# Splitting the log decays of a gated linear attention into three bf16 parts before their products with 0/1 matrices

## The reference, cut to what matters

```
z = einsum('bnsr,srk->bnsk', lr, w_gk) + b_gk
log_a = log_sigmoid(z) / GLA_GATE_NORM            # two directions, 4 heads x 64 channels
...
bc = cumsum(log_a within a chunk)
diff = bc[..., :, None, :] - bc[..., None, :, :]
decay = exp(where(causal, diff, -inf))
attn = sum(q[..., :, None, :] * k[..., None, :, :] * decay, axis=-1)
```

## Time and profile before

| | us |
|---|---|
| median of 3 runs (1561.78, 1561.84, 1566.01) | 1561.84 |
| the profiled execution | 1566.27 |
| its span, first to last instruction | 1564.6 |
| PE busy | 1421.5 (91%) |
| DVE busy | 425.7 (27%) |
| ACT busy | 261.4 (17%) |
| POOL busy | 133.6 (9%) |

### The profile page before, as it was taken

The page is one execution under the profiler, slowest core; times in us unless marked ns, Lnnn a source line. Parts: engine busy times, 40 slices in busy tenths (PEclk is TensorE's granted clock), DMA queues, the critical chain, the costliest instruction groups (busy, mean ns, idle before and its releaser), DMA issues. The chain is left out here.

```text
span 1564.6 us, 28137 instructions
## 1 busy us (share of the span) xinstructions
PE 1421.5 (91%) x11994; PEld 742.3 (47%) x11995; DVE 425.7 (27%) x1058; ACT 261.4 (17%) x489; POOL 133.6 (9%) x357
## 2 busy tenths in 40 slices
PE   3899988899999999999959998979998999999996
PEld 2675656434434434444446666554443444344442
DVE  2291774311111111111125538460111111111112
ACT  1313204211101111101113231141111111111110
POOL 2600631000000000000000026020000000000000
PEclk8899999899999999999979999979999999999998
DMA  6854950599999999999745679009999999999994
GB/s 248 276 186 173 362 185 1 234 420 420 420 420 409 416 420 420 421 415 421 325 161 177 239 267 318 29 7 421 421 421 420 421 418 413 414 400 421 420 416 177
DMA packets 114116, 507.48 MB, mean 324 GB/s; under 512 B 14880, under 2 KB 20796, under 8 KB 64572
## 3 DMA queue, kind: packets, MB, share of 16 engines
q1 hardware_dynamic: 113372, 504.43, 80.5%
q0 software_dynamic: 384, 1.05, 0.2%
q10 hardware_dynamic: 224, 0.06, 0.0%
HBM read 503.41 MB, written 2.10 MB: 323 GB/s over the span
## 5 line engine op out<-in xcount | busy, mean ns | idle before, releaser
L971 PE MATMUL ps<-ring,h 128*32 128x512 f32 x2720 | 374.8, 599 | 24.1 <-DMA ring<-in_exp_w_up 14.8
L971 PEld LDWEIGHTS ps<-ring,h 128*32 128x32 f32 x2720 | 109.3, 111 | 248.5 <-issue 248.5
L990 PE MATMUL ps<-ring,work 128*32 128x512 f32 x1360 | 199.6, 598 | 3.1 <-DVE store L1627 1.6
L971 PE MATMUL ps<-store,h 128*32 128x512 f32 x608 | 191.1, 619 | 9.4 <-issue 6.9
L997 PE MATMUL ps<-store,work 128*128 128x512 f32 x416 | 192.4, 605 | 1.6 <-DVE store L1635 1.6
L957 PEld LDWEIGHTS ps<-tm,work 128*128 128x128 bf16 x2496 | 144.4, 98 | 44.3 <-issue 43.1
L957 PE MATMUL ps<-tm,work 128*128 128x128 bf16 x2496 | 156.9, 219 | 0.3
L1625 DVE TENSOR_TENSOR work<-work,ps 128x256 f32<-128x256 f32 x52 | 21.9, 422 | 408.7 <-ACT work L1300 408.7
L997 PEld LDWEIGHTS ps<-store,work 128*128 128x128 f32 x416 | 74.7, 189 | 120.0 <-issue 116.5
L1627 DVE COPY store<-ps 128x512 f32<-128x512 f32 x52 | 36.0, 692 | 328.9 <-PE ps L990 328.9
L1300 ACT ACTIVATE work<-ps 128x256 f32<-128x256 f32 x52 | 20.0, 384 | 479.8 <-PE ps L971 479.8
(11 more groups left out here) (294 smaller groups left out, 1241.9 us busy)
## 6 DMA issues: line engine op xcount, KB each, us to landing
ring<-in_exp_w_gate SPq DMA_DIRECT2D x102, 1024.0 KB, 14.6
ring<-in_exp_w_up SPq DMA_DIRECT2D x102, 1024.0 KB, 17.0
ring<-in_exp_w_down SPq DMA_DIRECT2D x102, 1024.0 KB, 14.9
ring<-in_w_ada SPq DMA_DIRECT2D x28, 2048.0 KB, 10.6
store<-in_exp_w_gate SPq DMA_DIRECT2D x26, 1024.0 KB, 15.6
store<-in_exp_w_up SPq DMA_DIRECT2D x26, 1024.0 KB, 17.8
work<-in_exp_w_down SPq DMA_DIRECT2D x26, 1024.0 KB, 15.2
ring<-in_w_in SPq DMA_DIRECT2D x6, 2048.0 KB, 12.8
```

Of the source, the lines that this page charges most:

```text
L971: last = mm(ps[first:first + TILE, 4, :], X_e[:, b, kt, first:first + TILE], gate_up(slot, kt), start=(kt == 0), stop=(kt == KT - 1))
L990: last = mm(ps[first:first + TILE, 7, :], turn[:, P * j + first:P * j + first + TILE], down(slot, j, half), start=(j == 0), stop=(j == 1))
```

## The change

`la` is written as the sum of three bf16 tiles (`la3`), and the matrices `mf` and `mb` are stored as bf16. `decays(g)` runs three bf16 matmuls per bank in place of one f32 matmul, accumulating in PSUM. The first part is a bf16 copy of `la` by ACT, after `keep_ada(0)`. POOL subtracts it from `la` into `la_rest` (in f32, in the space of the softmax tile `p1`); ACT copies that to the second part, after `nT_ready`; POOL subtracts again, ACT copies the third part after the second sigmoid of the convolution and waits for it before the softmax. Two of the parts have a new tile, the third lies in a free stretch of `store`. The state product at L840 still reads the f32 `la`.

```diff
-    mf = sb("mf", [P, LEVELS + 1, P])
-    mb = sb("mb", [P, LEVELS + 1, P])
+    mf = sb("mf", [P, LEVELS + 1, P], BF16)
+    mb = sb("mb", [P, LEVELS + 1, P], BF16)
+    la_parts = sb("la_parts", [P, 2, STREAMS, 2, 256], BF16)
+    la3 = [la_parts[:, 0], la_parts[:, 1], la_low]
...
+    la_rest = p1.rearrange("p (s a) k -> p s a k", s=STREAMS)
...
                 for b in range(2):
-                    last = mm(bank(b), la[:, st, dr, P * a:P * (a + 1)],
-                              m[:, 4 * b:4 * (b + 1), :].rearrange("p l n -> p (l n)"), start=True, stop=True)
+                    for i, part in enumerate(la3):
+                        last = mm(bank(b), part[:, st, dr, P * a:P * (a + 1)],
+                                  m[:, 4 * b:4 * (b + 1), :].rearrange("p l n -> p (l n)"), start=(i == 0), stop=(i == 2))
...
             pe.wait_ge(s["pT_ready"], 1)
+            pe.wait_ge(s["la_part"], 3)
             decays(0)
...
             kept_all(I_NAX)
             keep_ada(0)
+            act.wait_ge(s["la_ready"], STREAMS)
+            nc.scalar.copy(la3[0], la).then_inc(s["la_part"], 1)
             kept_all(I_QK)
             keep_ada(1)
...
             nc.scalar.copy(kcT, bank(1, 0, 256).rearrange("p (a n) -> p a n", a=2)).then_inc(s["nT_ready"], 1)
+            act.wait_ge(s["la_rest"], 1)
+            nc.scalar.copy(la3[1], la_rest).then_inc(s["la_part"], 1)
             kept_all(I_V)
...
             nc.scalar.activation(csig, cacc[:].rearrange("p c s t -> p c (s t)"), ACT.Sigmoid)\
               .then_inc(s["conv_sig"], 1)
+            act.wait_ge(s["la_rest"], 2)
+            nc.scalar.copy(la3[2], la_rest).then_inc(s["la_part"], 1)
+            act.wait_ge(s["la_part"], 3)
             for st in range(STREAMS):
                 act.wait_ge(s["max_ready"], st + 1)
...
             nc.gpsimd.tensor_tensor(biasr, biasr, maskr[:].unsqueeze(1).broadcast_to([P, HEADS, P]), ALU.add)\
               .then_inc(s["bias_ready"], 1)
+            pool.wait_ge(s["la_part"], 1)
+            nc.gpsimd.tensor_tensor(la_rest, la, la3[0], ALU.subtract).then_inc(s["la_rest"], 1)
+            pool.wait_ge(s["la_part"], 2)
+            nc.gpsimd.tensor_tensor(la_rest, la_rest, la3[1], ALU.subtract).then_inc(s["la_rest"], 1)
             pool.wait_ge(s["small_in"], 16 * N_SMALL)
             pool.wait_ge(s["nq_ready"], 1)
```

More of the change, by code:

```diff
@@ L127 @@
 gate_in0 gate_in1 gate_in2 gate_in3 gate_in4 down_in0 down_in1 down_in2 down_in3 down_in4 act_step dve_step ada_done ada_kept bias_in square_done
-mod_shown mod_ready diag_ready hT_shown hT_ready vec_shown vec_ready proj_done proj_kept z_shown la_log la_ready
+mod_shown mod_ready diag_ready hT_shown hT_ready vec_shown vec_ready proj_done proj_kept z_shown la_log la_ready la_part la_rest
 conv_sig tap conv_ready convT_shown ctok_ready convB_shown conv_neg cact_ready pw_shown cat_conv nq_ready
@@ L171, in build @@
     gains = store[0:2 * KT, 2816:2944]
+    la_low = store[:, 2944:3456].bitcast(BF16).rearrange("p (s a n) -> p s a n", s=STREAMS, a=2)
     hT = store[:, 3584:5632].rearrange("p (k n) -> p k n", k=KT)
```

## The result

The changed kernel takes **1569.2 us** (median of 11 runs, 1566.88 to 1570.53). The kernel before, run beside it, reads 1563.1 (11 runs, 1561.78 to 1566.01). The ratio is **1.0035 [1.0026, 1.0044]**, so about 5.5 us slower; a second set of runs gave 1.0028 [1.0018, 1.0039]. The forecast was +2.2 us, and the measured time lies above its range. Of the distance between the two times, 1.3 us belongs to the kernel before: the three runs that the forecast started from had their median at 1561.84, and all eleven have it at 1563.1. The two profiled executions differ by less, 1568.88 against 1566.27 us, since that of before lies above the median of its runs; so the stretches of the mixing stage are compared, not the spans.

A forecast was written before the change was run, and what follows sets the result against it. The chain of waits was taken to bound the kernel, through DVE's convolution, PE's blocks before the GLA loop, and the loop. -2.0 + 3.6 + 0.6 = +2.2 us on 1561.84 gave 1564.0 us, range 1559.0 to 1568.3.

The forecast's parts named there:

- Gain, 2.0 us: Cheaper decays products: 0.43 us per call, 1.7 us from four calls on the path plus 0.3 from decays(7) in layer 1.
- `pairs` waits longer for DVE, as said: Sign in the GLA loop: DVE as releaser of pairs, with PE waits longer than 0.62 us.
- Loss, 3.6 us: Convolution: POOL's first subtraction holds DVE's taps, 1.8 us a layer, which delays PE by as much.
- A DVE instruction with two SBUF inputs stands still for most of a POOL instruction: Convolution taps beside POOL's 2.15 us subtraction: 0.83 of it lost, 1.8 us a layer.
- rival 1: Convolution taps not held by POOL's subtraction, only the gain left: 1559.8 us; chance 0.13.
- Clock, 0.6 us: After PE's longer wait for q and k, low clock in transposes and projection of v costs 0.3 us a layer.
- rival 2: Longer wait keeps PE slow longer in transposes and projection of v: 1.9 us a layer, 1567.2 us; chance 0.15.
- the decision point of 1.6 us a layer: Further clock loss behind PE's wait for q and k from which rival 2 decides.
- At those places PE's own speed decides nothing: GLA loop: PE mostly waits for DVE's mask, so cheaper decays(2) to decays(6) change nothing.

The follow-up runs named there:

- e1_split_later: The changed kernel with POOL's two subtractions moved behind the scaled keys and their two stores; ratio 0.9986 to the kernel before.
- e3_products_only: The changed kernel with only the first bf16 part made, the other two zeros, and no POOL subtractions; ratio 0.9985 to the kernel before.
- e2_split_only: The changed kernel's split, copies and waits, but products in f32 from the unsplit la with f32 matrices, parts unused; ratio 1.0031 to the kernel before.
- e4_delay_only: The kernel before with DVE's squares of q and k written one and a half times more; ratio 1.0029 to the kernel before.
- e7_gap_in_taps: The changed kernel with one convolution tap (number 50) waiting for all taps before it; 1569.03 us in a single execution.
- e9_change_loop_filled: The changed kernel with three f32 matmuls of constants in PE's wait before the pairs of group 5; ratio 1.0017 to the kernel before.
- e5_change_filled: The changed kernel with four f32 matmuls of constants before PE's wait for q and k; ratio 0.9990 to the kernel before.
- e6_later_filled: e1_split_later with two f32 matmuls of constants before PE's wait for q and k; ratio 0.9969 to the kernel before.
- r2_later_filled_again: e6_later_filled measured once more, on another chip; ratio 0.9972 to the kernel before.

## Why the prediction was wrong

- **Gain, 2.0 us: right in total, in part by luck.** 2.2 us (`e1_split_later`) and 2.3 (`e3_products_only`). A call gives 0.51 us and not 0.43, and within a call the bf16 matmuls start 0.21 us apart, as worked out. In layer 0 stretch C falls by 0.7 and 1.1 us in these two kernels, where the forecast had 0.9; in layer 1 by 1.9 in both, where it had 1.2. There 0.8 us come from the way from `pairs(5)` to `pairs(6)`, 7.18 us before and 6.3 in these two; that this is owed to the products is not shown. `pairs` waits longer for DVE, as said: 0.96 and 0.74 us in the changed kernel's loop where 0.51 and 0.20 stood.
- **Loss, 3.6 us: right in size, wrong in place.** "A DVE instruction with two SBUF inputs stands still for most of a POOL instruction" holds for the squares, not for the taps in a close row. The sign that I had named for rival 1, taps unchanged in total, was seen, and its time (1559.8) was not: the delay only moved to the next DVE instruction. The rows of before could not tell this apart, since in them POOL met DVE instructions most of which waited for the one before, with gaps of 0.02 to 0.04 us. The Trainium skill (GPSIMD Engine Reference, section Specifications) speaks of a shared interface with contention; the trace agrees (12.88 us in place of 2.14), but that the closely issued side wins, and for how long, only the trace told.
- **Clock, 0.6 us: the step that failed.** I took 0.3 us a layer "since the row shows the drop as complete at the present length". The row shows the level to which the clock had fallen, not when it comes back: in the changed kernel the return to full clock comes later after the longer wait, and the transposes and the projection of v take 0.65 to 1.14 us longer in a layer (stretch B: +2.6 and +1.5 us over the two layers). This is rival 2's mechanism at half its price, so the decision point of 1.6 us a layer was not reached there. The price is not fixed: of the twelve layers with a wait of 4.0 to 4.3 us (profiles of the changed kernel, `e2_split_only`, `e4_delay_only`, `e7_gap_in_taps` and `e9_change_loop_filled`) two show none of it.
- **What was not in the sum at all: the clock in the loop.** "At those places PE's own speed decides nothing" was read from PE's waits for DVE. But `pairs(5)` waits for POOL, and POOL does not wait for the products alone: PE, done sooner, rests longer there (2.22 us against 1.64 in layer 0, 2.83 against 2.25 in layer 1). Behind that rest the changed kernel does `pairs(5)` at the lower level, 1.5 us longer in layer 0 and 0.7 in layer 1; from `pairs(5)` to `pairs(6)` that makes 1.1 and 0.3 us more than before. That cheaper work turned into a longer rest is shown. That the longer rest brought the lower clock is not: `e1_split_later`, `e3_products_only` and `e5_change_filled` rest as long and pay nothing, and the kernel before pays in layer 1 after 2.25 us.

The sum by measured terms, for the two layers: +3.6 (squares) + 2.0 (clock after the wait, the mean of 2.6 and 1.5) + 1.4 (the loop, by `e1_split_later`'s C against that of the changed kernel, 2.6 - 1.2; by the second profile 2.7) - 2.2 (products) = +4.8 us, by the second profile +6.1, against 5.5 and 4.4 measured.

**Open.** Why `pairs(5)` meets the lower clock in all four layers of the changed kernel's two profiles, and in none of six in `e1_split_later`, `e3_products_only` and `e5_change_filled`, after waits of the same 2.2 to 2.8 us. In `e7_gap_in_taps` it does in one layer (3.32 us) and not in the other (1.83); in the kernel before, `e6_later_filled` and `r2_later_filled_again` it does in some layers too. The length of the wait does not decide it alone; nothing else was tried.

## What to carry to other kernels

Before giving POOL an instruction on two SBUF tiles, look not for the DVE instruction that runs beside it but for the first one after DVE's next pause, and ask who waits for that; moving the two subtractions behind the DVE chain was worth about 7 us here (1.0028 to 1.0035 against 0.9986). Price a lengthened PE wait as the wait plus some of the work behind it at the lower clock (here up to 1.1 us a layer more), and look for waits that other PE work, made cheaper, will lengthen. Where such a wait can't be shortened, matmuls of constants in it give the clock back: 0.27% on the kernel before, with nothing else changed.

## What the runs showed of the hardware

- **DVE taps issued closely keep POOL waiting for as long as they last**: 12.88 us for a subtraction of 2.14, ending 1.99 us after the last tap. A single pause (`e7_gap_in_taps`) lets it in, and DVE then pays 1.87 us.
- **The price of PE's rest.** After 2.2 to 2.5 us of waiting the blocks up to the `ada_step` take 16.65 or 16.66 us (kernel before, `e1_split_later`, `e3_products_only`, both layers of each). After 4.0 to 4.3 us they take 17.31 to 17.79 in ten layers. With matmuls of constants in the wait and 0.5 to 0.8 us of rest left they take 14.97 or 14.98. In two more layers the clock was still high when the wait of 4 us ended and fell only behind it, and the price stayed that of the short wait; `e2_split_only`, layer 1, 897.35 - 880.67 = 16.68 us:

```profile
880.67 1.09 PE L718 MATMUL ps<-ident,h 128*128 128x128 f32 x8 [4.04 <-DVE h L1430]
...
897.35 1.95 PE L327 MATMUL ps<-ring,cs 128*32 128x128 f32 x64
```

At 116 to 118 us the granted clock is 0.98 before (2.4 GHz nearly throughout; its wait ended 1.8 us sooner), 0.50 in the changed kernel (1.2 GHz), and in `e5_change_filled` 1.00:

```profile
114.00:116.00 2.00, 2.00 (x9) 1.04 (x7) 1.90 (x4) 1.61 (x4) 0.00 (x0) 1.00 1.04 355
...
116.00:118.00 2.00, 2.00 (x6) 0.86 (x5) 1.86 (x6) 0.86 (x1) 1.07 (x1) 1.00 1.05 401
```

The Trainium skill (TensorE: Matmul & The Clock Gate, Part 1) says that the low clock is the default and that sustained activity releases it; `e5_change_filled` agrees, since PE is kept at work there and the clock stays at 1.00 in these stretches.
